# A two-block transformer kernel: constant multiplies on TensorE inside each of the 15 norms

## The reference

```
for l in range(2):                                   # first block
    x = x + 0.5 * swiglu(rmsnorm(x, ffn1_norm[l]), ...)
    x = x + hybrid_mixer(rmsnorm(x, mix_norm[l]), ...)
    x = x + 0.5 * swiglu(rmsnorm(x, ffn2_norm[l]), ...)
x = rmsnorm(x, final_norm)
for l in range(2):                                   # second block
    x = layer_norm(ALPHA * x + 0.5 * swiglu_ffn(x, ...), ...)
    x = layer_norm(ALPHA * x + mixer_sublayer(x, ...), ...)
    x = layer_norm(ALPHA * x + memory_cross_attention(x, mem, ...), ...)
    x = layer_norm(ALPHA * x + 0.5 * swiglu_ffn(x, ...), ...)

def rmsnorm(x, g):    return x * rsqrt(mean(x * x) + 1e-6) * g
def layer_norm(x, g, b):
    mu = mean(x); var = mean((x - mu) ** 2)
    return (x - mu) * rsqrt(var + 1e-5) * g + b
```

## Time and profile before

| what | value |
|---|---|
| runs | 2999.47, 3001.38, 3002.86 us; median 3001.38 |
| span of the profiled execution | 3000.7 us |
| own time of that execution | the page gives none beside the span |
| PE, PEld busy | 94%, 90% of the span |
| DVE, ACT busy | 51%, 45% |
| mean granted TensorE clock | 0.931 of full |

### The profile page before, as it was taken

One profiled execution on the slowest core, in us unless ns is written; L12 is line 12 of the kernel. 1 busy time (PEld: TensorE's weight loads), 2 busy tenths in 40 slices (PEclk: granted clock), 3 DMA queues, 4 the chain that ended last, 5 costly groups with the idle time before them and its releaser, 6 DMA issues.

```text
span 3000.7 us, 51103 instructions
## 1 busy us (share of the span) xinstructions
PE 2806.1 (94%) x21314; PEld 2710.1 (90%) x21314; DVE 1540.7 (51%) x1724; ACT 1362.3 (45%) x1568; POOL 110.8 (4%) x147
## 2 busy tenths in 40 slices
PE   8999979999989799999999999899999899998998
PEld 8999979999989799899989789799899897897997
DVE  5445755455467654444437345454554464355543
ACT  5445434344365344444334654543443335545442
POOL 0001200000003000000000000000000000000000
PEclk9999989999999899999979999799899799998998
DMA  6454244454443344544523243254444332243342
GB/s 234 163 201 151 71 148 176 144 184 173 163 162 110 127 154 160 202 155 153 203 85 127 85 169 139 99 189 145 154 174 162 128 126 106 104 170 127 133 145 86
DMA packets 72724, 441.65 MB, mean 147 GB/s; under 512 B 8416, under 2 KB 10592, under 8 KB 34192
## 3 DMA queue, kind: packets, MB, share of 16 engines
q1 hardware_dynamic: 69408, 432.80, 40.7%
q0 software_dynamic: 1104, 4.35, 0.5%
q10 hardware_dynamic: 2080, 2.62, 0.2%
HBM read 437.12 MB, written 2.62 MB: 147 GB/s over the span
## 4 chain that ended last, share of the span: by engine, by line
PE 83%; DVE 7%; ACT 6%; issue 3%; DMA 0%; POOL 0%; DVEq 0%; ACTq 0%
PE acc L447 25%; PE acc L448 24%; PE acc L449 24%; ACT w_hi L359 4%; DVE w_lo L364 2%; PE stat L496 1%; PE stat L494 1%; PE bc L506 1%; DVE tmp L1326 1%; DVE tmp L1324 1%; PE acc L483 1%; PE acc L485 1%; PE acc L484 1%; DVE x_lo L1335 0%; PE aux L576 0%
## 5 line engine op out<-in xcount | busy, mean ns | idle before, releaser
L364 DVE TENSOR_TENSOR w_lo<-raw,w_hi 128x2048 fp32r<-128x2048 f32 (+2 forms) x474 | 946.7, 2009 | 819.7 <-ACT w_hi L359 819.3
L447 PE MATMUL acc<-x_hi,w_hi 128*128 128x256 f32 x4368 | 1280.0, 293 | 50.9 <-DVE x_lo L1601 18.7
L448 PE MATMUL acc<-x_lo,w_hi 128*128 128x256 f32 x4368 | 1261.9, 289 | 0.0
L449 PE MATMUL acc<-x_hi,w_lo 128*128 128x256 f32 x4368 | 1261.2, 289 | 0.0
L447 PEld LDWEIGHTS acc<-x_hi,w_hi 128*128 128x128 f32 x4368 | 863.4, 198 | 82.5 <-issue 42.8
L448 PEld LDWEIGHTS acc<-x_lo,w_hi 128*128 128x128 f32 x4368 | 867.3, 199 | 0.7 <-issue 0.5
L449 PEld LDWEIGHTS acc<-x_hi,w_lo 128*128 128x128 f32 x4368 | 865.3, 198 | 0.0
L359 ACT ACTIVATE w_hi<-raw 128x2048 fp32r<-128x2048 f32 (+2 forms) x474 | 785.6, 1671 | 81.5 <-PE acc L449 81.3
L447 PE MATMUL acc<-h_parts,w_hi 128*128 128x256 f32 x1408 | 399.3, 284 | 0.0
L448 PE MATMUL acc<-h_parts,w_hi 128*128 128x256 f32 x1408 | 399.0, 283 | 0.0
L449 PE MATMUL acc<-h_parts,w_lo 128*128 128x256 f32 x1408 | 399.0, 283 | 0.0
(11 more groups left out here) (326 smaller groups left out, 2539.9 us busy)
## 6 DMA issues: line engine op xcount, KB each, us to landing
raw<-in_w SPq DMA_DIRECT2D x298, 1024.0 KB, 4.8
raw<-in_w SPq DMA_DIRECT2D x128, 704.0 KB, 4.1
raw<-in_w SPq DMA_DIRECT2D x48, 512.0 KB, 3.3
skew<-tmp ACTq DMA_DIRECT2D x1, 1536.0 KB, 6.2
small<-in_small POOLq DMA_DIRECT2D x2, 754.0 KB, 4.9
x<-in_x SPq DMA_DIRECT2D x1, 1024.0 KB, 4.8
tmp<-skew ACTq DMA_DIRECT2D x1, 1024.0 KB, 6.7
tmp<-in_mem POOLq DMA_DIRECT2D x2, 512.0 KB, 6.5
```

The costliest lines, as they stand in the source:

```text
L364: nc.vector.tensor_tensor(w_lo[:, slot, 0:n], raw[:, slot, 0:n], w_hi[:, slot, 0:n].bitcast(F32), ALU.subtract).then_inc(lo_done, 1)
L447: nc.tensor.matmul(out, w_hi_, v_hi_, start=start, stop=False)
L448: nc.tensor.matmul(out, w_hi_, v_lo_, start=False, stop=False)
L449: return nc.tensor.matmul(out, w_lo_, v_hi_, start=False, stop=stop)
```

## The change

A function `keep_busy(n)` is added on PE. It multiplies the 128x128 identity by the 128x128 matrix of ones, both constant, n times into the first 128 columns of the first `aux` bank, which nobody reads at that time. It is called once per tile of the norm, behind the wait for the square and ahead of the sums; three times ahead of the wait for `diag`; and four times behind the `bc` matmul (not in norm 14).

```diff
+            def keep_busy(n):
+
+                for _ in range(n):
+                    nc.tensor.matmul(aux[:, 0, 0:P], ones[:, :], ident[:, :], start=True, stop=True)
+
             def norm(N):
 
                 for n in range(KD):
                     pe.wait_ge(sq_ready, KD * N + n + 1)
+                    keep_busy(1)
                     for tt in range(2):
                         if centred(N):
                             nc.tensor.matmul(stat[:, 2 * tt:2 * tt + 1], x[:, n, tt * P:(tt + 1) * P], mean_col[:, :],
...
                 if is_cross:
                     memory_keys(N, subs[:N].count("cross"), 0)
 
+                keep_busy(3)
                 width = 2 * S if centred(N) else S
                 pe.wait_ge(diag_ready, N + 1)
                 nc.tensor.matmul(bc[:, 0:width], ones[:, :], diag[:, 0:width], start=True, stop=True).then_inc(bc_done, 1)
+                if parts(N):
+                    keep_busy(4)
                 if is_cross:
                     memory_keys(N, subs[:N].count("cross"), 1)
                     memory_values(N)
```

## The result

The changed kernel takes 3024.4 us (3023.8 to 3026.4, 4 runs) where the kernel before takes 3001.4 (2999.5 to 3002.9). The ratio is 1.0075, with an interval of 1.0061 to 1.0090. It is slower by 18 to 27 us. I had forecast 3031, with a range of 3013 to 3038.

A forecast was written before the change was run, and what follows sets the result against it. The prediction took PE, busy 94% of the span, and mainly its weight matmuls to bound the kernel. 20.5 + 2.2 + 3.4 + 0.8 + 3.1 = 30.0 us on 3001.4 gave 3031 us, range 3013 to 3038.

The forecast's parts named there:

- Step 1: One multiply per tile ahead of its sums, 16 passes in each of 15 norms; 20.5 us over six centred norms.
- Norms 9 and 13: Sums behind the cross sublayer, partly covered: DVE's read 1.1 us later each, 2.2 us in all.
- Norm 0: Sums start at the slow pace and DVE waits for them: added multiplies cost 3.4 us.
- Norms 1, 3, 4, 6: Plain norms' added sum passes end before DVE's read, which stands behind two weight splits: cost 0.
- Norms 2 and 5: Sums behind mix1, shorter cover: 0.4 us each, 0.8 in all; norm 5, with no row shown, 0 to 3.4.
- Steps 2 and 3: Three multiplies ahead of `diag`, four behind `bc`: hidden, except 1.57 us each in norms 8 and 12, 3.1 in all.
- step 3: Four multiplies behind `bc`: a delay of 0.1 us made up at once, but 0.90 us each in norms 8 and 12.
- What the clock gives back: Clock may rise behind `bc` but falls again before the last tile; plain norms have at most about 0.5 us each.
- three signs of being wrong: Norm 10's sums at clock 1.00 throughout, added passes less than 0.2 us apart at half clock, or last half-clock stretch gone.
- The 14.2 us and 6.8 us of norm 10: Expected time from first sum pass to DVE's read, 14.2 instead of 10.8 us, and DVE's idle time, near 6.8.
- a clock that holds through the arriving tiles: Rival: sums cost as forecast, but the clock, raised behind `bc`, holds through the arriving tiles: 3017 us, chance 15%.
- The first rival: Clock stays full through the norms, sums, `bc` and last stretch get shorter: -32 us, 2969 us, chance 6%.

The follow-up runs named there:

- e1: Against the kernel before, only one constant multiply per tile ahead of its sums, in all 15 norms: 3021.5 us, ratio 1.0062.
- e4: Against the kernel before, one constant multiply per tile ahead of its sums only in plain norms 1 to 6: 3003.3 us, ratio 1.0000.
- e12: Against the kernel before, one-column sums kept, multiplies ahead of `diag`, behind `bc` and among arriving tiles, first four chunks outside the ffn's loop: 2991.9 us, ratio 0.9956.
- e7: Against the kernel before, one constant multiply per tile ahead of its sums in norm 0 alone: 3007.3 us, ratio 1.0010.
- e2: Against the kernel before, only the four constant multiplies behind the `bc` matmul: 3003.7 us, ratio 0.9999.
- e5: Against the kernel before, two constant multiplies per tile ahead of its sums, nothing else added: 3031.5 us, ratio 1.0097.
- e9: Against the kernel before, 128-column sums, multiplies ahead of `diag`, behind `bc` and among arriving tiles, first four chunks outside the ffn's loop: 2957.2 us, ratio 0.9846.
- e6: Against the kernel before, each sum pass streams 128 equal columns instead of one, no constant multiplies: 2973.3 us, ratio 0.9895.

## Why the prediction was right

- **Step 1 is the loss, and only where DVE waits for the sums.** Right in place: e1 has 18 of the 23 us, e4 nothing. Its size was too high. I had 3.41 us for each of six centred norms, and the traces show 2.94, 3.30, 1.55, 3.16, 3.35 and 1.60, together 15.9 instead of 20.5. I had taken the clock to fall where it fell before. In norms 10 and 14 it fell 5.2 us after the first pass instead of 3.2, so some 18 more passes ran at 0.112 instead of 0.213 us. Whether the added columns did that is not shown for one multiply per tile. For it: 5.2 here and 6.0 in e1 are later than in any kernel with one-column sums and nothing added to them. Against it: among those the fall in norm 10 moved too, from 2.3 (e12) over 3.2 (before, e7) to 4.8 us (e2), and norm 11 of the changed kernel, with the same passes, has 3.1. For two multiplies per tile e5 shows it in most norms.
- **Norms 9 and 13** cost 0.5 us each, not 1.1, since the clock fell there 4.4 us after the start instead of 3.0. **Norm 0** cost 3.4 us, as worked out.
- **Norms 1, 3, 4, 6** cost nothing, as said. Norms 2 and 5 cost nothing here, and e4 has 0.23 us of DVE's wait in norm 2.
- **Steps 2 and 3** were hidden except in norms 8 and 12, where 1.65 us each stand against the 1.57 worked out. For step 3, e2 bears it out.
- **What the clock gives back.** It rose behind `bc` in norms 10 and 11 and fell again among the tiles, as I had it. In norms 7, 9 and 13 it did not rise there at all. The plain norms gave back the 1.35 us that my sum had left at nothing.
- **The signs.** None of the three signs of being wrong came: norm 10's sums were at half clock for 7.1 us, the added passes there were 0.21 us apart, and the last stretch was at 0.50. The 14.2 us and 6.8 us of norm 10 came out as 12.33 and 4.93; norm 11 has 14.26 and 6.87.
- **Luck.** 30.0 us were forecast and 22 to 23 measured. That 3024 lies in the range is owed to its low end, which I had drawn for another reason, a clock that holds through the arriving tiles. Between a fall where it was before and no fall at all I had no case.
- **The first rival, that the clock stays full,** fell for this kernel. What separates it from e9, where the clock does stay full in most centred norms, is where the columns are: in the sum passes and among the arriving tiles, not ahead of the sums.

What stays open is why the fall came 5.2 us into the sums in norms 10 and 14 and 3.1 us in norm 11 of the same kernel, with the same passes in each, and why it moves between kernels in sums that nobody changed. The stretches show where it fell, not what decided it.

## What to carry to other kernels

If TensorE's clock falls while the engine works without a gap, look at what its instructions stream, not only at whether it is busy. Here 127 more columns in each sum pass cost no time (0.112 us a pass as before; more than 128 columns were not tried) and gave 1% (e6: 0.9895), and a separate constant matmul was free only in a wait that something else ends. Before adding one, look for who waits for the instruction behind it, and whether the place is in a loop's body.

## What was not expected of the hardware

A float32 pass streaming 128 columns takes the same 0.112 us in a row of such passes as one streaming a single column (64 passes in 7.3 us, e6, at full clock). With one column each, 64 passes without a gap ran at granted clock 1.00 for 3.2 us and 0.50 for 7.6 us (e7); with 128 they ran at 1.00 to the end. And the clock then held through 2.1 us of idle time and `bc` (e6, norm 10), although PE did nothing in that wait. In norm 11 of the same kernel it fell within the wait, and `bc` ran at half clock (2.06 us busy).
